# Attention weights scaled before their product, mixer outputs produced turned, and the scatter moved behind the second expert product, in a one-layer decoder kernel

## What is computed

```python
mod = jax.nn.silu(c) @ ada_w + ada_b                  # six modulation vectors
sh1, sc1, g1, sh2, sc2, g2 = jnp.split(mod[:, None, :], 6, axis=-1)
h = (_rms(x, norm1_g) * (1.0 + sc1) + sh1).astype(dtype)
z = h @ w_in                                          # split into q, k, v, gates of m, b, r, n
p_c = e_c / jnp.maximum(jnp.sum(e_c, axis=-1, keepdims=True), 1e-30)
o_cmp = jnp.einsum('bhtn,bhnd->bhtd', p_c, v_cmp)
...
p = jax.nn.softmax(s, axis=-1)                        # o_slc, o_win, and the whole of b, alike
return from_heads(g[0] * o_cmp + g[1] * o_slc + g[2] * o_win)
...
y = jnp.concatenate([y_m, y_b, y_r, y_n], axis=-1).astype(dtype) @ w_out
x = x + g1 * y
h2 = (_rms(x, norm2_g) * (1.0 + sc2) + sh2).astype(dtype)
return x + g2 * hier_moe(h2, ...)    # per token: gate-weighted (silu(x w1) * (x w3)) w2 of 2 experts
```

## Time and profile before

| | us |
|---|---|
| median of 3 runs | 1700.9 |
| lowest, highest | 1700.34, 1703.17 |
| the profiled execution's own time | 1700.04 |
| its span, first to last instruction | 1698.2 |
| PE busy | 1356.3 |
| DVE busy | 549.4 |

### The profile page before, as it was taken

How to read it: one execution, slowest core, us unless ns; L and a number is a source line. 1 busy time by engine, 2 the same in 40 slices (tenths; PEclk the granted TensorE clock), 3 DMA queues, 4 the chain that set the end, 5 groups by cost and what they waited for, 6 DMA issues and landing times.

```text
span 1698.2 us, 28260 instructions
## 1 busy us (share of the span) xinstructions
PE 1356.3 (80%) x12797; PEld 860.5 (51%) x12797; DVE 549.4 (32%) x901; ACT 129.0 (8%) x280; POOL 27.3 (2%) x30
## 2 busy tenths in 40 slices
PE   5999999999999999997766676667666666666757
PEld 4664547855456854574543443534435334344434
DVE  3554564664456353132120221121120221211203
ACT  2000100101101100130000000000000000000000
POOL 0000000000000000010000000000000000000000
PEclk9999999999999999999987887887888888788889
DMA  9999776668657775738999999999999999999995
GB/s 397 426 426 383 295 306 260 264 245 325 228 217 275 291 289 221 323 149 363 426 426 426 426 426 426 427 426 428 425 427 426 426 427 426 426 426 426 426 427 236
DMA packets 44616, 613.21 MB, mean 361 GB/s; under 512 B 4896, under 2 KB 5168, under 8 KB 6736
## 3 DMA queue, kind: packets, MB, share of 16 engines
q1 hardware_dynamic: 42848, 604.00, 86.0%
q0 software_dynamic: 1072, 6.44, 0.9%
q10 hardware_dynamic: 576, 0.88, 0.2%
HBM read 609.21 MB, written 2.10 MB: 360 GB/s over the span
## 4 chain that ended last, share of the span: by engine, by line
DMA 52%; PE 43%; DVE 3%; issue 1%; SPq 0%; POOL 0%; ACT 0%; DVEq 0%
DMA ring<-in_exp_w 24%; DMA Zpad<-in_exp_w 23%; PE W L607 16%; PE W L599 7%; DMA ring<-in_stream 6%; PE W L900 5%; PE M L983 4%; PE W L876 2%; PE A L1007 1%; PE W L956 1%; DVE ada_s L1281 1%; PE W L943 1%; PE M L583 1%; PE W L573 1%; PE A L564 1%
## 5 line engine op out<-in xcount | busy, mean ns | idle before, releaser
L607 PE MATMUL W<-ring,buf_h 128*128 128x512 f32 x704 | 307.6, 596 | 3.8 <-DMA ring<-in_stream 3.8
L983 PE MATMUL M<-ring,g1b 128*32 128x128 f32 x4608 | 172.1, 311 | 108.2 <-DMA ring<-in_exp_w 98.1
L983 PEld LDWEIGHTS M<-ring,g1b 128*32 128x32 f32 x4608 | 149.4, 126 | 143.1 <-DMA ring<-in_exp_w 123.2
L607 PEld LDWEIGHTS W<-ring,buf_h 128*128 128x128 f32 x704 | 132.9, 191 | 165.2 <-issue 165.1
L1281 DVE SCALAR_TENSOR_TENSOR ada_s<-ring,small,ada_s 128x512 f32<-128x512 f32 x236 | 177.5, 752 | 8.4
L1744 DVE SCALAR_TENSOR_TENSOR tmp<-tmp,M 128x128 f32<-128x128 f32 x32 | 9.2, 288 | 481.3 <-ACT tmp L1198 481.3
L983 PE MATMUL M<-Zpad,g1b 128*32 128x128 f32 x2560 | 108.6, 341 | 67.4 <-DMA Zpad<-in_exp_w 36.3
L1220 DVE TENSOR_TENSOR consts<-A,g2b 32x512 f32<-32x512 f32 x128 | 87.9, 687 | 204.7 <-PE A L1007 201.7
L983 PEld LDWEIGHTS M<-Zpad,g1b 128*32 128x32 f32 x2560 | 94.8, 139 | 84.5 <-DMA Zpad<-in_exp_w 41.0
L599 PE MATMUL W<-buf_h,ring 128*128 128x256 f32 x512 | 113.7, 383 | 0.8 <-DMA ring<-in_stream 0.8
L599 PEld LDWEIGHTS W<-buf_h,ring 128*128 128x128 f32 x512 | 97.8, 192 | 14.4 <-issue 1.0
(11 more groups left out here) (293 smaller groups left out, 941.8 us busy)
## 6 DMA issues: line engine op xcount, KB each, us to landing
ring<-in_exp_w SPq DMA_DIRECT2D x104, 2048.0 KB, 36.0
ring<-in_stream SPq DMA_DIRECT2D x88, 2048.0 KB, 9.1
Zpad<-in_exp_w SPq DMA_DIRECT2D x64, 2048.0 KB, 37.1
PPY<-in_exp_w SPq DMA_DIRECT2D x24, 2048.0 KB, 35.8
Zpad<-in_early SPq DMA_DIRECT2D x8, 1536.0 KB, 10.6
buf_x<-in_x SPq DMA_DIRECT2D x2, 1024.0 KB, 7.0
buf_h<-in_x POOLq DMA_DIRECT2D x1, 2048.0 KB, 12.3
out<-buf_h SPq DMA_DIRECT2D x4, 512.0 KB, 3.0
```

The lines of the kernel that those rows point to most:

```text
L607: ins = pe.matmul(dst[:, tt * 512:tt * 512 + 512], hT[:, kk, tt * P:tt * P + P], w[:, 512 * k:512 * k + 512], start=(kk == 0), stop=(kk == ...
L983: ins = pe.matmul(M[32 * c:32 * c + 32, 512 * w13:512 * w13 + 128], XT[:, kk, 32 * q:32 * q + 32], w[:, 512 * k + 128 * c:512 * k + 128 * ...
```

## The change

- `ORDER`: the modulation block 8 no longer stands ahead of the first chunk; every block up to 21 takes the place of the one after it, and blocks 22 and 23 stand behind the first and the second quarter of the output projection (`ADA_BEHIND`). `gates` stands between the halves of the first chunk.
- Attention weights are divided by their sums (times the branch's gate) in PA ahead of `turn_p`, by DVE: 2 small instructions and 2 of 128x1024 and 128x512. PE's `turn_p` waits for them (`p_scaled`). For blocks 14 and 20 (`LATE_HALF`) DVE does the first half at the block's place, and the second half only behind this scaling. The compressed branch's 128x120 weights are scaled likewise.
- `pv` and `cmp_pv` swap their operands, so that the result has head elements on partitions and tokens along the row, as YT needs it. The branches of n are added in YT; ACT copies b there. `turn_y` of n and of b are gone.
- In the first gather and in the loop the tokens are gathered in 4 parts in place of 2, and ACT and DVE dress alternate parts.
- In q = 0 of the loop, PE's `scatter` and the turning of the gates stand behind the w2 product.
- In the router two small DVE subtractions (`group_arg`, `pair_arg`), which ACT waits for ahead of its copy of g2, stand behind the expert mask.

```diff
-ORDER = [('extras', 0), ('blocks', 0), ('ada', 8),
-         ('chunk', 'n_ks'), ('gates', 0), ('cmp_hid', 0), ('norm', 'n_q'), ('ada', 9),
...
-         ('chunk', 'm_v'), ('pv', 'slc'), ('ada', 15), ('scores', 'win'),
-         ('chunk', 'm_o'), ('turn_p', 'win'), ('ada', 16), ('pv', 'win'),
-         ('chunk', 'b_v'), ('m_decay', 0), ('ada', 17), ('turn_y', 'n'),
...
+ORDER = [('extras', 0), ('blocks', 0), ('gates', 0),
+         ('chunk', 'n_ks'), ('cmp_hid', 0), ('norm', 'n_q'), ('ada', 8),
...
+         ('chunk', 'm_v'), ('pv', 'slc'), ('ada', 14), ('scores', 'win'),
+         ('chunk', 'm_o'), ('turn_p', 'win'), ('ada', 15), ('pv', 'win'),
+         ('chunk', 'b_v'), ('m_decay', 0), ('ada', 16),
...
+LATE_HALF = {'win': 14, 'moba': 20}
...
                 elif step == 'cmp_pv':
...
+                    for h in range(H):
+                        ins = pe.matmul(M[:, h * T:h * T + T], vc[0:N_CMP, h * DH:h * DH + DH],
+                                        PB[0:N_CMP, h * T:h * T + T], start=True, stop=True)
...
                 elif step == 'turn_p':
-                    pe.wait_ge(sem["exp_done"], n_att)
+                    pe.wait_ge(sem["p_scaled"], n_att)
...
-                        pe.matmul(M[:, d], pt[:, 0:P], v[:, d], start=True, stop=True)
-                        o1 = M[:, 512 + h * DH:512 + h * DH + DH]
-                        pe.matmul(o1, pt[:, P:2 * P], v[:, d], start=True, stop=False)
-                        ins = pe.matmul(o1, pt[:, 2 * P:3 * P], v[:, 512 + h * DH:512 + h * DH + DH],
-                                        start=False, stop=True)
+                        pe.matmul(o, v[:, d], pt[:, 0:2 * P], start=True, stop=False, skip_group_check=True)
+                        ins = pe.matmul(o[:, P:T], v[:, 512 + h * DH:512 + h * DH + DH], pt[:, 2 * P:3 * P],
+                                        start=False, stop=True, skip_group_check=True)
...
-                        if q == 0:
-
-                            scatter(it)
...
+                        pe.wait_ge(sem["hh_ready"], 4 * it + q + 1)
+                        if q == 1:
                             pe.wait_ge(sem["gt_ready"], it + 2)
...
+                        if q == 0:
+
+                            scatter(it)
+
+                            pe.wait_ge(sem["hT_ready"], 4 * it + 1)
...
-                if step == 'ada':
+                if step == 'ada' and arg in LATE_HALF.values():
+                    ada_half(arg, 0)
+                elif step == 'ada':
                     ada_accumulate(arg)
...
+                    for tt, p in ((1, PA[:, 0:1024]), (0, PA[:, 1024:1536])):
+                        ins = tt_op(p.rearrange("p (h t) -> p h t", h=H), p.rearrange("p (h t) -> p h t", h=H), bc(fac[:, 4 * tt:4 * tt + 4], p.shape[1] // H), ALU.mult)
+                    ins.then_inc(sem["p_scaled"], 1)
+                    if arg in LATE_HALF:
+                        ada_half(LATE_HALF[arg], 1)
...
-                        tt_op(tth(tmp[:, 0:1024]), tth(M[:, 0:1024]), bc(fac, DH),
-                                ALU.mult).then_inc(sem["o_read"], 1)
-                        dve.wait_ge(sem["o_read"], n_att)
-                        ins = tt_op(yb, yb, tmp[:, 0:1024], ALU.add)
+                    ins = tt_op(yT_n, yT_n, M[:, 0:1024], ALU.add).then_inc(sem["o_read"], 1)
```

198 lines of the change are left out of this document (103 added, 95 removed).

## The result

The changed kernel takes 1706.3 us (median of 8 runs, 1702.3 to 1709.1), and 1706.6 us in five more later on. The kernel before took 1701.8 us beside the first of these. The ratio is 1.0030, with a 95% interval of 1.0019 to 1.0041: slower by 4 to 5 us, a little over the 0.2% that a measurement can tell. I had forecast 1701.5 us, with no change as the likeliest (0.50) and slower at 0.28; the measured time lies near the upper end of the range that I gave, 1694 to 1707 us.

A forecast was written before the change was run, and what follows sets the result against it. PE bounds the kernel up to the router, transfers the experts behind it. Terms of -9.0, +13.5 and -3.9 sum to +0.6 us on the profiled 1700.04; with the runs' median 0.9 higher, the forecast is 1701.5 us, range 1694 to 1707.

The forecast's parts named there:

- The front: First chunk: no wait for its load, -3.8; no low clock behind it, -1.7; no wait for DVE's gate reading, -1.3 us.
- The margin of 0.4 us at n_vs: At chunk n_vs, whose load was to land just in time with 0.4 us to spare; taken as 0.
- The wait for b_v: Ahead of chunk b_v, PE waits because block 14's late half holds its buffer, +9.2; slower clock behind that, +1.7 us.
- Two sums in a row: Behind b_v, the sums of blocks 14 and 15: a wait for DVE, +0.4, and one more clock loss, +1.7 us.
- The clock at 303 us: Half chunk behind the compressed product, 15.77 us at low clock: the loss was kept unchanged, with a bound of -1.7 us.
- The turned products: Attention: two times 8 transposes go, -1.8 us; fewer instruction starts in the products, -0.4, bounds 0 and -0.8.
- The router: ACT copies g2 later because its exponential's operand is made behind the mask, so PE's gather begins +0.5 us later.
- The first group: First expert group: w2 ahead of the scatter frees its buffer by about 778, closing a landing gap: -3.9 us.
- The tail: Behind the last expert half's landing: 14 us of products, addition and store, with no change forecast.

The follow-up runs named there:

- Experiment 6: The kernel before, with only block 8 moved from the front and the gates put between the first chunk's halves: 1693.0 us, ratio 0.9966.
- Experiments 1 to 3: The changed kernel with block 14 left whole: 1695.7 us; both its halves behind the scaling: 1713.8; its late half exchanged with m_o's first half in the stream: 1693.7.
- scatter_back: The changed kernel with the scatter and the turning of the gates put back ahead of the w2 product: 1706.4 us, ratio 1.0025.
- experiment 5: The changed kernel with block 14 read whole ahead of the scaling, its sum between b_v's halves, and the two router steps back in place: 1691.4 us, ratio 0.9947.
- scatter_only: The kernel before, with only the scatter and the turning of the gates moved behind the w2 product: 1698.4 us, ratio 0.9985.
- quarters_only: The kernel before, with only the gathered tokens dressed in quarters, ACT and DVE taking alternate ones: 1698.9 us, ratio 0.9993.
- after_again: The changed kernel once more, unchanged, for a second profile and more times: 1706.6 us, ratio 1.0040.
- order_only: The same run as Experiment 6: the kernel before with block 8 and the gates moved, nothing else; 1693.0 us.
- order_loop: The kernel before, with block 8 and the gates moved and both expert-loop edits (scatter behind w2, quarters), attention as before: 1690.2 us, ratio 0.9937.

## Why the forecast was 4 us too low

The forecast of the time was 4.8 us too low, of which 0.9 is the kernel before, whose median was that much higher beside the changed one. The change itself was +4.5 us where I had +0.6. The terms one by one:

**The front** (-3.8, -1.7, -1.3): right. Experiment 6 gives 6 to 8 us for it. The margin of 0.4 us at n_vs became a wait of 0.52 in after and 1.08 in experiment 6, which I had taken as 0.

**The wait for b_v** (+9.2, +1.7): right in place, cause and size. Measured 9.14 and 9.20. PE was ready at 391.0, the late half ended at 392.2, the load took 7.76 us, as the 7.8 of the earlier trace rows. (The Trainium skill, DMA: Bandwidth & Descriptors, "Anatomy of one DMA", gives its formula for transfers that GpSimd issues. By it the load would take 6.8 us, an estimate; SP issues this one, and the measured 7.76 us decides.) Experiments 1 to 3 show the cause: the wait is gone with the block whole, goes from 9.14 to 15.09 us with twice the late work, and is gone when only the buffer is another. The clock loss inside the half was 1.5 to 1.8 us in the two profiles of after and 3.1 in scatter_back (16.97).

**Two sums in a row** (+0.4, +1.7): the wait is right at 0.35. The clock's part was mis-sized: 1.8 to 4.9 us, mostly 3.4, and experiment 5 gives 3.5 for parting the sums and moving the router's steps together.

**The clock at 303 us** (kept): wrong for after, whose half chunk takes 14.08 us and not 15.77. All five kernels with before's form of the compressed product have that loss, and of the nine with the new form, whose code is the same up to there, four have it. So what I took for fixed is in good part chance; whether the form has a share these counts do not show. It is 1.7 us in the other direction.

**The turned products** (-0.4, and -1.8 for `turn_y`): the compressed product takes 1.99 us against 1.97, so it gained nothing. The three attention products take 2.78 to 2.86 us where they took 2.84 to 2.92: -0.2 together, where I had -0.4 with the compressed one. The 16 transposes of `turn_y` are gone from PE's timeline; their -1.8 has no experiment of its own.

**The router** (+0.5): PE waits 1.18 us for the copy of g2 where before had 0.67. Right, less 0.15 us, since PE waits 1.37 us for the mask where it waited 1.52.

**The first group** (-3.9): mis-sized. The hole closed, but that the refill stands at 777.53 where I had said 778 is luck: 778 was in the times of before, and the gather came 3.1 us later. Behind the gather the refill comes 3.6 us sooner than I had reckoned, for the most part because DVE's 0.85 us and the stop of 2.2 us are gone, neither of which I had counted. The time from the gather to the last half fell by only 1.9. Of the 2.0 that are missing, 0.4 stand between the gather and the first expert landings. The rest is further on: among the later landings some come late, 20 by some 0.8 us each before, 11 by 1.5 us in the changed kernel, which cost 1.6 us more together. I had left them out. This goes with the attention's edits and not with the loop's (the last section has the count). And I gave the scatter's move the whole credit, where the quarters alone take 2.4 us off the hole. I had written that the finer dressing brings 0 there.

**The tail** (0): 17.2 us in the first profile, 14.1 in the second. This is no term of the change, but a profile that has it lies 3 us above one that has not.

Sum: before the gather +3.1 and +6.6 in the two profiles, where I had +4.5; behind it -1.9 where I had -3.9; the tail +3.1 and 0. In the first profile the 3.8 us over my +0.6 are 2.0 of the first group and 3.1 of the tail, less 1.4 up to the gather, where the missing loss at 303 us helped. In the second the 4.2 us are 2.1 of the first group and 2.1 up to the gather: 3.2 more of clock behind the two sums, less the 1.7 at 303 us, and small things. So the forecast had its largest term right by its mechanism. The worth of the closed hole is off by 2 us the same way in both profiles, and the rest of the 4 us is clock, which differs from profile to profile.

## What to carry to other kernels

In a ring of buffers, read a late half not by the time of the engine that reads it but by who stands five places on: DVE had 10 us to spare, and the same late work cost 9 us in one buffer and nothing in its neighbour's. When a step is split so that another comes sooner, look at what else of it is queued ahead of that other one: here the end of a sum, not the bulk of the work. And a hole in the queue of transfers is worth what the sum of the landings says, and not its own length: 3.9 us of it brought 1.9 here.

## What the runs showed of the hardware

In these profiles low clock is a matter of chance and cause together. With the same code, the granted clock behind the two sums was 0.66 over 5 us in one profile and 0.53 over 11 us in the other (two levels, 1.2 and 2.4 GHz), which moves the gather by 3 us; the wait of 3.76 us ahead of the first chunk was followed by a chunk of 29.40 us in before and 29.31 in scatter_only, and of 27.70 in quarters_only. One profile therefore can't size such a term; a count over several kernels that share the code gives its spread. The windows of after and of after_again, and the first chunk in quarters_only:

```profile
436.00:441.00 5.00, 5.00 (x10) 2.04 (x9) 4.55 (x12) 1.70 (x2) 0.00 (x0) 0.66 0.50 213
```

```profile
434.00:445.00 11.00, 11.00 (x22) 5.83 (x22) 6.80 (x17) 1.69 (x2) 0.00 (x0) 0.53 0.40 167
```

```profile
139.14 27.70 PE L607 MATMUL W<-ring,buf_h 128*128 128x512 f32 x64 [3.76 <-DMA ring<-in_stream]
```

Behind the landing at 788.6 of before, and its like in the others, 179 expert halves land, and what they take over 4.89 us each adds up to 17.6 to 17.9 us in the nine profiles that have the changed attention. It is 16.1 to 16.4 in the five that have not (less the hole, wherever it stands), whether they come as 20 short ones (before, order_only, scatter_only, quarters_only) or mostly as 11 long ones (order_loop and the nine). The page counts 116 packets in the queue that carries instructions for the nine, and 109 or 110 for the five. The sum and PE's stop of 2.0 to 2.8 us in the first group thus both go with the size of the program, but no run changes that size by itself, so that it is the cause is a guess. The line of the page, of after and of order_loop (packets, MB, share):

```profile
q8 instruction: 116, 1.90, 0.5%
```

```profile
q8 instruction: 109, 1.79, 0.4%
```
